# First stage of a decoder-layer kernel: who asks for which tile, and when

## The reference

```
mk, mv = split(rms_norm(mem_prompt, mem_norm) @ w_mem_kv)      # 256 memory tokens
h = rms_norm(x, norm_pre)                                       # 1024 prompt rows, 8 sample rows
proj = h @ w_in                                                 # width 1024, 15 slices of w_in
k_all = concat(k_past[page_table], c_k)                         # 32 pages of 128 keys for each sample
z = q . k_all / sqrt(64) + bias                                 # stick-breaking attention
A = sigmoid(z) * prod(1 - sigmoid(z later))
```

## Time and profile before

| | |
|---|---|
| median of 3 runs | 1549.67 us |
| the profiled execution's own time | 1545.77 us |
| its span in the trace | 1544.1 us |
| TensorE busy | 1281.7 us (83%) |
| VectorE busy | 855.3 us (55%) |
| ScalarE busy | 481.0 us (31%) |
| GpSimd busy | 357.4 us (23%) |
| mean granted TensorE clock | 0.913 |

### The profile page before, as it was taken

The page is one execution under the profiler, slowest core; times in us unless marked ns, Lnnn a source line. Parts: engine busy times, 40 slices in busy tenths (PEclk is TensorE's granted clock), DMA queues, the critical chain, the costliest instruction groups (busy, mean ns, idle before and its releaser), DMA issues. The chain is left out here.

```text
span 1544.1 us, 23048 instructions
## 1 busy us (share of the span) xinstructions
PE 1281.7 (83%) x7717; PEld 1073.5 (70%) x7717; DVE 855.3 (55%) x1192; ACT 481.0 (31%) x901; POOL 357.4 (23%) x235
## 2 busy tenths in 40 slices
PE   4577679889798854998988889599999997697997
PEld 4567557767676543888888788477777876366885
DVE  3245689888887532759779596243444443324221
ACT  4231245435445531232232413231313131322110
POOL 0029434424330000735434353000000000000000
PEclk8698789999899986999999999799999898898999
DMA  4446657557473423655354642475646452543320
GB/s 150 143 151 191 186 160 242 180 175 245 142 231 111 150 77 95 216 160 182 107 179 128 213 151 70 142 238 153 205 141 207 152 158 71 196 136 110 109 82 28
DMA packets 200276, 237.89 MB, mean 154 GB/s; under 512 B 13395, under 2 KB 122290, under 8 KB 200154
## 3 DMA queue, kind: packets, MB, share of 16 engines
q1 hardware_dynamic: 196194, 224.60, 46.8%
q0 software_dynamic: 3968, 11.87, 2.1%
HBM read 215.87 MB, written 20.64 MB: 153 GB/s over the span
## 5 line engine op out<-in xcount | busy, mean ns | idle before, releaser
L1979 POOL TENSOR_TENSOR bp_keys<-bp_keys,bp_q 128x1024 f32<-128x1024 f32 x64 | 156.4, 2465 | 171.7 <-DMA bp_keys<-cache_sb_k 163.9
L1979 POOL TENSOR_TENSOR cp_keys<-cp_keys,cp_q 128x1024 f32<-128x1024 f32 x64 | 161.5, 2542 | 142.9 <-DMA cp_keys<-cache_sb_k 139.7
L150 PE MATMUL bank<-xh,b_w_hi 128*128 128x344 f32 x480 | 163.0, 340 | 31.0 <-DVE b_w_lo L133 27.1
L150 PE MATMUL bank<-xl,b_w_hi 128*128 128x344 f32 x480 | 158.8, 331 | 0.0
L150 PE MATMUL bank<-xh,b_w_lo 128*128 128x344 f32 x480 | 158.4, 330 | 0.0
L150 PE MATMUL bank<-xh,d_w_hi 128*128 128x344 f32 x384 | 130.8, 341 | 26.0 <-ACT d_w_hi L128 18.3
L244 PE MATMUL bank<-xh,c_w_hi 128*128 128x344 f32 x384 | 130.6, 340 | 9.2 <-ACT c_qT L250 4.6
L244 PE MATMUL bank<-xh,c_w_lo 128*128 128x344 f32 x384 | 126.7, 330 | 0.0
L244 PE MATMUL bank<-xl,c_w_hi 128*128 128x344 f32 x384 | 126.7, 330 | 0.0
L150 PE MATMUL bank<-xl,d_w_hi 128*128 128x344 f32 x384 | 125.9, 328 | 0.0
L150 PE MATMUL bank<-xh,d_w_lo 128*128 128x344 f32 x384 | 125.8, 328 | 0.0
(11 more groups left out here) (376 smaller groups left out, 2603.1 us busy)
## 6 DMA issues: line engine op xcount, KB each, us to landing
cp_keys<-cache_sb_k SPq DMA_DIRECT2D x128, 256.0 KB, 2.8
cp_values<-cache_sb_v SPq DMA_DIRECT2D x128, 256.0 KB, 2.8
bp_keys<-cache_sb_k SPq DMA_DIRECT2D x128, 256.0 KB, 3.1
dp_values<-cache_sb_v SPq DMA_DIRECT2D x128, 256.0 KB, 3.0
b_w_raw<-w_in SPq DMA_DIRECT2D x20, 512.0 KB, 4.9
c_w_raw<-w_in SPq DMA_DIRECT2D x16, 512.0 KB, 5.1
d_w_raw<-w_in SPq DMA_DIRECT2D x16, 512.0 KB, 5.3
o_mix<-mix SPq DMA_DIRECT2D x8, 1024.0 KB, 5.9
```

The lines of the kernel that those rows point to most:

```text
L150: last = self.nc.tensor.matmul(self.bank(j, c)[:, 0:self.width], w[:, s, k, :], x[:, k, c * self.width:(c + 1) * self.width], start=(k == ...
L1979: self.nc.gpsimd.tensor_tensor(self.keys[:, s], self.keys[:, s], q, ALU.mult).then_inc(self.scaled.sem, 1)
```

## The change

1. Row blocks 3 to 10 are asked for by GpSimd, each with the same wait as before; SyncE asks for blocks 0 to 2 only. GpSimd's writes of heads 0 and 1 stand between these requests, those of heads 2 and 3 between its key products.
2. The query's weights are asked for right after memory tile 1. The query is computed in the turn of row block 4, and its eight products go to four column groups of the array (output partitions 0, 32, 64, 96), two products to each. VectorE copies the bank, and in the turn of block 5 one product with a 0/1 matrix (`fold`) adds the four groups.
3. Projection tiles M + 1 and M + 2 land in the two buffers of the memory tiles, so tiles M, M + 1 and M + 2 have a buffer each. SyncE asks for two key pairs, tiles 7 and M, two key pairs, tiles M + 1 and M + 2, and so on.
4. The first stage multiplies and reduces 12 of sample 0's 16 key pairs. The last four, the bias and the softplus are in the first two pieces of the second stage, and sample 1's query and first key pairs, and tile M + 4, are asked for at its beginning.
5. The turns of the memory heads stand one row block later.

```diff
+FIRST_KEYS = 12
...
+    def raw_of(self, j):
+
+
+
+        return j % 2 if j < self.memory else j - self.memory - 1 if j - self.memory in (1, 2) else 2
+
+    def source(self, j):
+        return self.raw[:, 0] if self.raw_of(j) == 2 else self.memory_raw[:, self.raw_of(j)]
+
     def load(self, sp, j, columns):
 
-        first = 2 if j < self.memory else self.memory + 1
-        if j >= first:
-            earlier = j - 1 if j < self.memory else j
-            sp.wait_ge(self.hi_ready, earlier)
-            sp.wait_ge(self.lo_ready, earlier)
+        earlier = [t for t in range(j) if self.raw_of(t) == self.raw_of(j)]
+        if earlier:
+            sp.wait_ge(self.hi_ready, earlier[-1] + 1)
+            sp.wait_ge(self.lo_ready, earlier[-1] + 1)
         sp.sem_inc(self.loading, 1)
-        if j < self.memory:
-            sp.dma_start(self.memory_raw[:, j % 2], columns).then_inc(self.memory_landed[j % 2], 16)
-        else:
-            sp.dma_start(self.raw[:, 0], columns).then_inc(self.landed, 16)
-
-    def source(self, j):
-        return self.memory_raw[:, j % 2] if j < self.memory else self.raw[:, 0]
+        sp.dma_start(self.source(j), columns).then_inc(self.landed[self.raw_of(j)], 16)
 
     def split_hi(self, act, j):
-        if j < self.memory:
-            act.wait_ge(self.memory_landed[j % 2], 16 * (j // 2 + 1))
-        else:
-            act.wait_ge(self.landed, 16 * (j - self.memory + 1))
+        act.wait_ge(self.landed[self.raw_of(j)], 16 * sum(self.raw_of(t) == self.raw_of(j) for t in range(j + 1)))
...
-    QUERY_ROW = SAMPLE + 5
-    head_of = lambda r: (r - SAMPLE - 3) // 2 if (r - SAMPLE - 3) % 2 == 0 and r >= SAMPLE + 3 else None
+    QUERY_ROW, FOLD_ROW = SAMPLE + 2, SAMPLE + 3
+    head_of = lambda r: (r - SAMPLE - 4) // 2 if (r - SAMPLE - 4) % 2 == 0 and r >= SAMPLE + 4 else None
+
+    def load_row(queue, r):
+        src, n, _, _, _ = row_tiles[r]
+        if r >= R:
+            queue.wait_ge(normed_done, r - R + 1)
+            queue.sem_inc(loading, 1)
+        queue.dma_start(rows[0:n, r % R, :], src).then_inc((first_in if r < R else rows_in)[r % R], 16)
 
     with nc.Block() as block:
 
         @block.sync
         def _(sp):
-            def load_row(r):
-                src, n, _, _, _ = row_tiles[r]
-                if r >= R:
-                    sp.wait_ge(normed_done, r - R + 1)
-                sp.dma_start(rows[0:n, r % R, :], src).then_inc(rows_in[r % R], 16)
-
-            def load_keys(i, first, end):
+            def load_keys(first, end):
                 for r in range(first, end):
-                    keys.load_keys(sp, i, r)
-
-            load_row(0)
+                    keys.load_keys(sp, 0, r)
+
+            load_row(sp, 0)
             sp.dma_start(gain_b[:, 1, :], k.mem_norm.to_broadcast([P, DM])).then_inc(gain_in[1], 16)
-            load_row(1)
-            load_row(2)
+            load_row(sp, 1)
+            load_row(sp, 2)
             c.load_tile(sp, k, 0)
             sp.dma_start(gain_b[:, 0, :], k.norm_pre.to_broadcast([P, DM])).then_inc(gain_in[0], 16)
             c.load_tile(sp, k, 1)
-            for r in range(3, NR):
-                load_row(r)
-                if r - 1 < M:
-                    c.load_tile(sp, k, r - 1)
-                if r == 6:
-                    sp.dma_start(w_query, k.w_in[:, :, C_Q:C_Q + GW]).then_inc(w_query_in, 16)
-                if r == 8:
-                    c.load_tile(sp, k, M)
+            sp.dma_start(w_query, k.w_in[:, :, C_Q:C_Q + GW]).then_inc(w_query_in, 16)
+            for j in range(2, M - 2):
+                c.load_tile(sp, k, j)
             keys.setup_sync(sp)
             sp.wait_ge(q_scaled, 1)
             sp.dma_start(k.q_dram, keys.q[0:NB, :]).then_inc(q_out, 16)
-            load_keys(0, 0, 4)
+            c.load_tile(sp, k, M - 2)
             sp.wait_ge(q_out, 16)
             keys.load_query(sp, 0)
+            load_keys(0, 2)
+            c.load_tile(sp, k, M - 1)
+            c.load_tile(sp, k, M)
+            load_keys(2, 4)
             c.load_tile(sp, k, M + 1)
-            load_keys(0, 4, 6)
             c.load_tile(sp, k, M + 2)
-            load_keys(0, 6, 12)
+            load_keys(4, 10)
             c.load_tile(sp, k, M + 3)
-            load_keys(0, 12, keys.PAIRS)
-            keys.load_query(sp, 1)
-            load_keys(1, 0, 4)
-            c.load_tile(sp, k, M + 4)
+            load_keys(10, FIRST_KEYS + 4)
...
+                if r == QUERY_ROW:
                     dve.wait_ge(q_summed, 1)
-                    nc.vector.tensor_scalar(keys.q[0:NB, :], QSUM[0:NB, :], SCORE_SCALE, None, ALU.mult).then_inc(q_scaled, 1)
+                    nc.vector.tensor_copy(partial[:], QSUM[:, :]).then_inc(q_copied, 1)
+                if r == FOLD_ROW:
+                    dve.wait_ge(q_folded, 1)
+                    nc.vector.tensor_scalar(keys.q[0:NB, :], QFOLD[0:NB, :], SCORE_SCALE, None, ALU.mult).then_inc(q_scaled, 1)
...
-            reduce_keys(4, 10)
+            reduce_keys(4, 8)
             stream.split_lo(dve, M + 3)
-            reduce_keys(10, keys.PAIRS)
-            keys.add_bias(dve, 0)
-            keys.softplus(dve, 0)
+            reduce_keys(8, FIRST_KEYS)
 
         @block.gpsimd
         def _(pool):
             k.fill(pool)
             keys.setup_pool(pool)
-            for h in range(MLH):
+
+            def write_memory(h):
                 pool.wait_ge(m_tok, 2 * h + 2)
                 pool.sem_inc(sending, 1)
                 columns = slice(h * P, (h + 1) * P)
                 pool.dma_start(k.mem_k[:, :, columns], k_tok[:, h % 2]).then_inc(m_out[h % 2], 16)
                 pool.dma_start(k.mem_v[:, :, columns], k.mem_v_tok[:, h]).then_inc(m_out[h % 2], 16)
-            for r in range(keys.PAIRS):
+
+            for r in range(R, NR):
+                load_row(pool, r)
+                if head_of(r - 2) is not None:
+                    write_memory(head_of(r - 2))
+            for r in range(4):
+                keys.multiply_keys(pool, 0, r)
+            for h in range(2, MLH):
+                write_memory(h)
+            for r in range(4, FIRST_KEYS):
...
+                pe.wait_ge(q_scaled, 1)
                 pe.wait_ge(m_tok, 2 * h)
                 for n, src in enumerate((k.mem_kT[:, h], vT[:, h % 2])):
                     for b in range(2):
@@ -515,13 +528,19 @@
                     turn_memory(head_of(r))
                 if r == QUERY_ROW:
                     pe.wait_ge(x_new_ready, 1)
+                    pe.wait_ge(cleared, 1)
                     pe.wait_ge(w_query_in, 16)
                     for kk in range(KT):
-                        last = nc.tensor.matmul(QSUM[0:NB, :], x_new[:, kk, :], w_query[:, kk, :], start=kk == 0, stop=kk == KT - 1)
+                        g = 32 * (kk % 4)
+                        last = nc.tensor.matmul(QSUM[g:g + NB, :], x_new[:, kk, :], w_query[:, kk, :], start=(kk < 4),
+                                                stop=(kk >= 4), skip_group_check=True)
                     last.then_inc(q_summed, 1)
+                if r == FOLD_ROW:
+                    pe.wait_ge(q_copied, 1)
+                    pe.wait_ge(k.filled, k.FOLD_SET)
+                    nc.tensor.matmul(QFOLD[0:NB, :], k.fold[:], partial[:], start=True, stop=True).then_inc(q_folded, 1)
...
+            load_tile(4)
+            load_keys(0, FIRST_KEYS + 4, NP)
             values.setup_sync(sp)
+            load_query(1)
+            load_keys(1, 0, 4)
             load_values(0, 0, 4)
...
+                if g == 1 or u == NU - 1 and i + 1 < GT:
                     load_tables(nc, act, LN_EXP)
-                    keys.softplus_tail(act, i + 1)
+                    keys.softplus_tail(act, 0 if g == 1 else i + 1)
...
+                if g == 0:
+                    reduce_keys(0, NP - FIRST_KEYS)
+                    keys.add_bias(dve, 0)
...
+            for r in range(FIRST_KEYS, NP):
+                keys.multiply_keys(pool, 0, r)
```

24 lines of the change are left out of this document (12 added, 12 removed).

## The result

| | before | after |
|---|---|---|
| median, runs | 1550.24 us, 4 | 1507.82 us, 4 |
| lowest to highest | 1547.23 to 1551.20 | 1506.40 to 1508.73 |
| profiled execution's own time | 1545.77 us | 1507.03 us |
| span | 1544.1 us | 1505.3 us |
| barrier after the first stage | 165.5 | 116.4 |

The ratio is 0.9739, 95% interval 0.9720 to 0.9758: 42.4 us less. In the traces the first stage is 49.1 us shorter, the second 10.4 us longer, and what follows it is as long as before (978.7 and 978.8): 38.8 us in all. The forecast was 61 less and 12 more.

What follows compares the result with a forecast made beforehand. The first stage was taken as bound by late row-block requests, with nothing overlapped in 10.75 us rounds. First stage 61 us less, second 12 more: 49 less, giving 1500.7 us; likeliest range 1491 to 1511, 8 in 10 between 1487 and 1520.

Steps and rivals of the forecast that it cites:

- likeliest case: Whole kernel: first stage 61 us shorter, second 12 longer, 1500.7 us; chance 0.55, own range 1491 to 1511.
- signs of being wrong: Turns of 6 us or more, low TensorE clock, SyncE or GpSimd last before the barrier, or second stage as long as before.
- The loop: First stage, row blocks 4 to 10: early requests leave the compute loop as limit, 4.35 us a turn, 30.5 for seven.
- Block 9: Row block 9's request stands behind head 0's writes in GpSimd's order, so ScalarE loses 4.5 us once; bounds 0 and 8.
- The query: Query products in four column groups cost 2.1 to 2.4 us, plus about 1 for copy, folding and wait; upper bound 7.03.
- GpSimd beside VectorE: Turns 9 and 10: GpSimd's first four key products delay VectorE by about 3 us, bounds 0 to 5.
- First projection product: End of the row loop: the terms sum to 68.2 us for its start, where it was at 105.9 before.
- Projection: With three tile buffers, 216 products take 34.8 us, to 103.0, where the projection took 44.7 before.
- The end of the stage: Key chain hidden, some 6 us ahead of TensorE; stage ends at 104.4 instead of 165.5, 1.4 us after TensorE.
- Second stage: Moved key reductions, bias, softplus and waits for sample 1's products add 12 us on VectorE; bounds 5.6 and 20.
- the key chain ends the stage: Rival, chance 0.07: first stage's key chain 15 us longer than counted passes TensorE by 8 us; 1509 us.
- slow loop: Rival, chance 0.15: in the row-block loop tiles land late or TensorE's clock stays low; about 1516 us, at worst 1524.

Runs made afterwards that it cites:

- e5: Kernel before with only GpSimd's requests for row blocks 3 to 10 and its writes of heads 0 and 1 added; 1518.0 us, ratio 0.9799.
- e2: Changed kernel with GpSimd's writes of heads 0 and 1 moved behind its request for row block 10; 1497.4 us, ratio 0.9669.
- e6: Changed kernel with SyncE asking for the rows, earlier in its order, and GpSimd only for the writes of heads 0 and 1; 1495.3 us.
- e10: Changed kernel with GpSimd waiting for its own result after each of the first four key products; 1499.6 us, ratio 0.9671.
- e9: Changed kernel with the first four key products split into 16 instructions of 256 columns; 1508.8 us, ratio 0.9749.
- e7: Changed kernel with all 16 key pairs' products and reductions ahead of the barrier, bias and softplus still behind it; 1508.0 us, ratio 0.9731.
- e11: e6 with the eight page requests of pairs 12 to 15 moved from before the barrier to the second stage's beginning; 1495.6 us, ratio 0.9652.

## Why the prediction was right, step by step

The forecast was 49 us less; 42.4 were measured in the medians and 38.8 between the two traces, and 1507.8 us lies inside the likeliest case's own range. Its parts are further off than its sum: the first stage gave 49.1 us where 61 were forecast. Of its signs of being wrong one came true, SyncE as the last engine before the barrier; the others did not (turns of 6 us, a clock under 0.8 between 30 and 68, where it was 0.89, a second stage as long as before). Of its signs of being right the first and last projection product and the barrier are missed by 8 to 12 us. By its steps:

- **The loop.** Forecast 4.35 us a turn. From block 5 to block 8, 24.43 to 38.56, three turns took 14.1 us with the query and its fold among them, where the forecast makes it 3 x 4.35 + 3.3 = 16.4; from block 9 to 10 it is 3.78. The mechanism was right, and the turn somewhat too long. e5 shows that this step alone is three quarters of the gain.
- **Block 9.** Forecast 4.5 us, measured 7.0. The mechanism was right: in e2 and e6 the wait is gone. The request went out at 41.90, about as forecast, but ScalarE was ready at 42.78 instead of 44.6, and the block came at 49.78, 7.9 us after the request was begun.
- **The query.** Forecast 2.1 to 2.4 us at about 27.7, measured 1.90 at 27.72.
- **GpSimd beside VectorE.** This is the term that was mis-sized, beyond its own bounds. Forecast 3 us (0 to 5), from a low part of 2.52 in the earlier trace rows; measured 10.16 - 1.22 = 8.9. I took from that row that VectorE loses one GpSimd instruction at a time, and it did there; at tile 7 it lost four. A wait between the products restores the old size (3.29 in e10), shorter products do not (11.15 in e9).
- **First projection product.** Forecast 68.2, measured 76.42. Block 10's statistics start at 53.56, within half a microsecond of what the forecast's terms give (24.3 + 5 x 4.35 + 3.3 + 4.5 = 53.9): the 2.5 us more at block 9 are made good by the shorter turns. The 8.2 us are all behind it, 5.9 in the low part and 2.5 in the products of tile 7, which the forecast had at 2.8 us and which took 5.31 at a clock of 0.55. The likeliest case had no term for the clock after a stall. With GpSimd's gaps alone the product is at 66.68, 9.7 us earlier, more than the 6.9 us that the low part gained.
- **Projection.** Forecast 34.8 us without a pause, measured 35.76.
- **The end of the stage.** Forecast 1.4 us after TensorE, with the key chain 6 us ahead and a cover that I called thin. Its last reduction was 0.3 us ahead, and its requests ended 3.15 us after TensorE: barrier 4.2 us after TensorE's last product. Most of the cover went because the chain was late by more than TensorE; and the last request is not beside the last reduction, where I put it, but 3.5 us behind: eight requests take 7.66 us from 107.68 on. In eleven of the fourteen kernels of the table the barrier comes 0.99 to 1.04 us after SyncE's last request, in e6 1.4, in e7 1.02 after VectorE, in e11 1.8 after TensorE. The kernel before is one of the eleven: its SyncE ended at 164.54 and its barrier was at 165.53.
- **Second stage.** Forecast 12 us more, measured 10.4, and VectorE waited for pair 1's product in its first piece as told. The working is confirmed for its place and its sum: the delay is 11.9 us at the third piece's first scan and changes by less than 2 us behind it. Of its parts, the four pairs with what waited behind them are 5.8 us (e7, 24.3 against 30.1); e7 still asks for sample 1's query and keys after the barrier, and the other 6.1 us go with that, with the bias or with the softplus, which no run tells apart. That e7's stage as a whole is no shorter comes from a wait for values and a lower clock 107 us into it, where e5, with nothing of the change in this stage, loses 3.7 of its 4.7 us as well (11.7 us against 8.0 in the kernel before).

The forecast of the time came out close because the errors of the first stage, 8.2 + 1.0 + 2.8 = 12.0 us, are small beside 61. They were all to one side, and nothing in the working made sure that they would stay that small. The rival "the key chain ends the stage" happened too, as a part of the likeliest case: 2.8 us, not 8. One sum of the rivals does not follow: half of the slow loop's 23 us on 1500.7 gives 1513, not 1516; no chance hangs on it.
